# Two transformer blocks in one launch: gate and up of the first block's feed-forward with the tokens stationary

## What is computed

```
def rms_norm(x, g):
    y = xf * lax.rsqrt(jnp.mean(xf * xf, axis=-1, keepdims=True) + NORM_EPS)
    return (y * g)

def swiglu_ffn(h, w_in, w_out):
    gate, up = jnp.split(h @ w_in, 2, axis=-1)
    return (jax.nn.silu(gate) * up) @ w_out

for l in range(DEPTH):                                   # DEPTH = 2
    x = x + 0.5 * swiglu_ffn(rms_norm(x, ffn1_norm_g[l]), ffn1_w_in[l], ffn1_w_out[l])
    ...                                                  # mixing, cross-attention
    x = x + 0.5 * swiglu_ffn(rms_norm(x, ffn2_norm_g[l]), ffn2_w_in[l], ffn2_w_out[l])
```

## Time and profile before

| | us |
|---|---|
| median of 3 runs | 2745.47 |
| profiled execution, its own time | 2742.86 |
| span of its trace | 2740.9 |
| PE busy | 2630.0 |
| DVE busy | 1700.7 |
| ACT busy | 1028.4 |
| four feed-forwards: down(0) of each ended at | 52.0, 635.7, 841.8, 1427.8 |

### The profile page before, as it was taken

How to read it: one execution, slowest core, us unless ns; L and a number is a source line. 1 busy time by engine, 2 the same in 40 slices (tenths; PEclk the granted TensorE clock), 3 DMA queues, 4 the chain that set the end, 5 groups by cost and what they waited for, 6 DMA issues and landing times. The chain is left out here.

```text
span 2740.9 us, 44687 instructions
## 1 busy us (share of the span) xinstructions
PE 2630.0 (96%) x18787; PEld 2324.0 (85%) x18787; DVE 1700.7 (62%) x2283; ACT 1028.4 (38%) x1275; POOL 99.2 (4%) x179
## 2 busy tenths in 40 slices
PE   8999989999989999989999999999999999989999
PEld 7999888989989999779899954355799899737999
DVE  6887655768768877656678822553455455354555
ACT  4335302444343354204443321643333333264333
POOL 2110000001101100000001000000000000000000
PEclk9999989999999999989999999889999999999999
DMA  8775201647766764004557752100355555210452
GB/s 277 261 260 185 93 1 47 200 140 244 261 216 223 264 224 154 16 1 138 171 174 258 260 193 77 46 1 31 127 183 183 199 184 185 78 62 31 140 183 93
DMA packets 279510, 415.63 MB, mean 152 GB/s; under 512 B 10105, under 2 KB 235721, under 8 KB 277698
## 3 DMA queue, kind: packets, MB, share of 16 engines
q1 hardware_dynamic: 260332, 348.16, 38.5%
q0 software_dynamic: 18128, 64.20, 6.8%
q10 hardware_dynamic: 902, 1.15, 0.1%
HBM read 399.82 MB, written 13.65 MB: 151 GB/s over the span
## 5 line engine op out<-in xcount | busy, mean ns | idle before, releaser
L614 PE MATMUL ps<-h_high,w_high 128*128 128x256 f32 x1984 | 567.9, 286 | 17.5 <-DVE w_low L1407 10.5
L616 PE MATMUL ps<-h_high,w_low 128*128 128x256 f32 x2016 | 572.3, 284 | 0.0
L614 PEld LDWEIGHTS ps<-h_high,w_high 128*128 128x128 f32 x1984 | 382.8, 193 | 20.3 <-DVE w_low L1407 11.4
L616 PEld LDWEIGHTS ps<-h_high,w_low 128*128 128x128 f32 x2016 | 389.0, 193 | 0.0
L1407 DVE TENSOR_TENSOR w_low<-ring,w_high 128x2048 fp32r<-128x2048 f32 x132 | 302.3, 2290 | 138.5 <-ACT w_high L1150 138.2
L615 PE MATMUL ps<-h_low,w_high 128*128 128x256 f32 x1312 | 373.4, 285 | 0.0
L2797 DVE TENSOR_TENSOR w_low<-ring,w_high 128x2048 fp32r<-128x2048 f32 x96 | 220.0, 2292 | 240.6 <-ACT w_high L2581 240.4
L1150 ACT ACTIVATE w_high<-ring 128x2048 fp32r<-128x2048 f32 x132 | 252.3, 1915 | 266.7 <-DMA ring<-in_ffn_w_in 147.9
L2581 ACT ACTIVATE w_high<-ring 128x2048 fp32r<-128x2048 f32 x96 | 183.8, 1916 | 331.2 <-PE ps L2260 304.1
L615 PEld LDWEIGHTS ps<-h_low,w_high 128*128 128x128 f32 x1312 | 254.0, 194 | 0.0
L1428 DVE SCALAR_TENSOR_TENSOR mod_acc<-wmod,cond,mod_acc 128x512 f32<-128x512 f32 x336 | 230.8, 748 | 0.0
(11 more groups left out here) (426 smaller groups left out, 5395.0 us busy)
## 6 DMA issues: line engine op xcount, KB each, us to landing
ring<-in_w_mlp SPq DMA_DIRECT2D x96, 1024.0 KB, 5.5
ring<-in_ffn_w_in SPq DMA_DIRECT2D x88, 1024.0 KB, 8.8
wmod<-in_w_mod POOLq DMA_DIRECT2D x96, 512.0 KB, 6.3
ring<-in_ffn_w_out SPq DMA_DIRECT2D x44, 1024.0 KB, 5.1
ring<-in_w_mix_in SPq DMA_DIRECT2D x26, 1024.0 KB, 5.5
ring<-in_xattn_w_kv SPq DMA_DIRECT2D x16, 1024.0 KB, 5.3
mod_scratch<-mod_acc POOLq DMA_DIRECT2D x24, 512.0 KB, 5.5
ring<-mod_scratch SPq DMA_DIRECT2D x12, 1024.0 KB, 6.8
```

The costliest lines, as they stand in the source:

```text
L614: mm(dst, w_hi, x_hi, start=start, stop=False, **more)
L616: return mm(dst, w_lo, x_hi, start=False, stop=stop, **more)
```

## The change

Gate and up are made the other way round. The tokens are stationary (`g_high`, `g_low`, 128 tokens at a time) and the weights move, gate and up side by side, 512 wide. The result has tokens on the partitions, so silu, 1/rms (now a column, `root_col`, one number per partition) and the product with up are done there in two halves of 128 tokens; then PE turns the product back with four transposes (`turn`), ACT makes its high part out of PSUM (`cast`) and DVE its low part (`act_lower`). All 11 steps use x times gain; the normed h of the feed-forward and its splitting fall away, the sums of squares come out as columns. High parts have five buffers: a pair for each half b of gate and up, which must lie so that one access pattern spans both, and one for down (`DOWN_HIGH`, in the place of `h_high`). `sync_program` is not touched.

```diff
+GATE_UP_HIGHS, DOWN_HIGH = ((0, 1), (6, 2)), 7
...
+            def half_products(b, t, k, last=False):
+                out = ps[4 + 2 * b + t].rearrange("p (r n) -> p r n", r=2)
+                toks, cols, s = slice(t * P, (t + 1) * P), slice(k * BLK, (k + 1) * BLK), tiles.slot(0, b)
+                hi, lo = gate_up_high[b][:, :, cols], w_low[:, s:s + 2, cols]
+                mm(out, g_high[:, k, toks], hi, start=(k == 0), stop=False)
+                mm(out, g_high[:, k, toks], lo, start=False, stop=False)
...
+            def turn(i, b):
+                pe.wait_ge(*tiles.act(i, 2))
+                for t in range(2):
+                    for m in range(2):
...
+                        last = nc.tensor.transpose(ps[4 + 2 * b][:, m * T + t * P:m * T + (t + 1) * P],
+                                                   act_tok[:, at:at + P], ident)
...
+            with pe.Fori(1, FFN_STEPS // 2 - 1) as j:
+                gate_up(1, j * 6 + 2)
+                down(j * 2, 0, j * 6 + 4)
+                turn(j * 2 + 1, 1)
+                gate_up(0, j * 6 + 5)
+                down(j * 2 + 1, 1, j * 6 + 7)
+                turn(j * 2 + 2, 0)
...
+                silu(j * 2, 0, j)
+                w_high_part(tiles, 2, 0, j, DOWN_HIGH, (2, 1, j - 1))
+                cast(j * 2, 0)
+                gate_up(0, j + 1, (1, 0, j))
...
+            silu(2 * j + 2, 0, j + 1)
+            w_high_part(tiles, 2, 0, j + 1, DOWN_HIGH, (2, 1, j))
+            cast(2 * j + 2, 0)
...
+            def rest(i, b, down_at, chunk, gate_up_at):
+                k = 4 * b
+                modulate(l, f, chunk, range(k, k + 1))
+                w_low_of(2, b, down_at, DOWN_HIGH)
+                act_lower(i, b)
+                modulate(l, f, chunk, range(k + 1, k + 2))
+                if gate_up_at is not None:
+                    w_low_of(0, b, gate_up_at, GATE_UP_HIGHS[b][0])
+                modulate(l, f, chunk, range(k + 2, k + 3))
+                if gate_up_at is not None:
+                    w_low_of(1, b, gate_up_at + 1, GATE_UP_HIGHS[b][1])
+                modulate(l, f, chunk, range(k + 3, k + 4))
```

More of the change, by code:

```diff
@@ L619, in ffn, with parts @@
             tiles = FfnTiles(l, f)
-            def parts(r, b, t, buffer):
+            def parts(b, t):
                 pe.wait_ge(*tiles.split(t, w_low_ready))
[L624 to L638, removed]
-                    last.then_inc(w_used[tiles.slot(r, 0)].sem, 1)
+                return [ap.rearrange("p (k n) -> p k n", k=2)
+                        for ap in (w_high[DOWN_HIGH], w_low[:, tiles.slot(2, b), :])]
@@ new lines, in half_products @@
+            def half_products(b, t, k, last=False):
[4 more added lines that the diff above has]
+                mm(out, g_high[:, k, toks], lo, start=False, stop=False)
+                if not last:
+                    return mm(out, g_low[:, k, toks], hi, start=False, stop=(k == KD - 1))
+                for r in range(2):
+                    mm(out[:, r, :], g_low[:, k, toks], hi[:, r, :], start=False, stop=(r == 1)
+                       ).then_inc(w_used[tiles.slot(r, b)].sem, 1)
@@ L675, in down, with tiles_half, gate_up @@
-            def down(i, b, t, buffer):
-                hi, lo = parts(2, b, t, buffer)
+                    for t in range(2):
+                        for k in (2 * p, 2 * p + 1):
+                            last = half_products(0, t, k, t == 1 and k == KD - 1)
+                        if t == 0 and p == KD // 2 - 1:
+                            last.then_inc(*tiles_half())
+            def tiles_half():
+                return half_done.sem, 1
+            def gate_up(b, t, between=None):
+                pe.wait_ge(*tiles.split(t + 1, w_low_ready))
+                for half in range(2):
+                    for k in range(KD):
+                        last = half_products(b, half, k, half == 1 and k == KD - 1)
+                    if half == 0:
+                        last.then_inc(*tiles_half())
+                        if between:
+                            between()
@@ new lines, in turn, with down @@
+            def turn(i, b):
+                pe.wait_ge(*tiles.act(i, 2))
+                for t in range(2):
+                    for m in range(2):
+                        at = b * 512 + t * BLK + m * P
+                        last = nc.tensor.transpose(ps[4 + 2 * b][:, m * T + t * P:m * T + (t + 1) * P],
+                                                   act_tok[:, at:at + P], ident)
+                last.then_inc(act_turned.sem, 1)
+            def down(i, b, t, between=None):
+                hi, lo = parts(b, t)
@@ L1183, in ffn, with silu, gate_up @@
-            silu(FFN_STEPS - 1, 0, FFN_STEPS // 2, True)
-            w_high_of(2, 0, FFN_STEPS // 2, 2, (0, 0, FFN_STEPS // 2))
+            def silu(i, b, use):
+                for t in range(2):
+                    act.wait_ge(*(tiles.used(1, b, use) if t else tiles.step(i, half_done)))
+                    at = t * BLK
+                    go(prob[:, b, at:at + BLK], ps[4 + 2 * b + t][:, 0:BLK], SILU, scale=root_col[:, t:t + 1]
+                       ).then_inc(silu_done.sem, 1)
+            def gate_up(b, use, before=None):
+                for r in range(2):
+                    w_high_part(tiles, r, b, use, GATE_UP_HIGHS[b][r], before)
```

295 lines of the change are left out of this document (135 added, 160 removed).

## The result

The changed kernel takes **2842.77 us** (median of four, 2829.82 to 2850.81) against 2745.44 for the kernel before: ratio 1.0349, 95% interval [1.0308, 1.0390], 97 us slower. The forecast of 2808 had the side and the place right; its range ended at 2836, so the time lies outside it.

What follows compares the result with a forecast made beforehand. PE alone was taken to set the 17.28 us step, waiting on a load chain after the change. Steps with clock +54, ends +17 and heads -8 gave +63 us: 2806 profiled, 2808 as median, range 2765 to 2836.

Steps and rivals of the forecast that it cites:

- the 512-wide matmul: PE's gate and up: 0.2144 us each, 10.29 against 11.52 a step; with transposes a step of 16.49, gaining 0.79.
- the landing of up: SP's load of up arrives 13.2 us after a down's end instead of 12.46, delayed by POOL's pieces.
- the clock: PE at 1.2 GHz behind long waits in the steps: 1.5 us for each of four, +6 us a feed-forward.
- DVE's wait for `mod_free`: DVE's k = 0 modulation waits 5.4 us for POOL's store; taken as harmless since DVE has room.
- E10: End of a feed-forward's tenth down, put at 163.0 us after the first down's end, without the clock; before, 155.5.
- the stated recurrence: Each down ends 16.49 us after the later of the last down's end and the one before plus 20.0; +7.5 a feed-forward.
- I take half a piece more: POOL's 512 KB pieces ahead of gate and up take 1.4 us each; half a piece added makes the landing 13.2.
- Ends and heads: Around the feed-forwards: ends +17 us, including 5.0 us waits before the last down; heads -8 us.
- The dearer matmul with more of POOL's traffic in front: Rival in the steps: 512-wide matmuls at 0.2267 us and a 21 us load chain, 2836 us; 8 in 100 including matmul price alone.
- its lesser form: Rival in gate and up: only the 512-wide matmuls dearer, at 0.2267 us, 2820 us; within the same 8 in 100.
- PE still sets the step: Rival in the steps: up lands early enough that PE does not wait, 2726 us; 5 in 100.
- The overlap at 0.12: Rival in gate and up: 512-wide matmuls start 0.12 us apart, gate_up 5.8 us, total 2714; 1 in 100.

Runs made afterwards that it cites:

- experiment 5: Changed kernel with POOL's modulation-weight loads, from the third on, moving 16 columns a row instead of 512: 2807.23 us, ratio 1.0259.
- Experiment 4: Changed kernel with DVE's k = 0 modulation put behind down's and the activation's low parts in every second step: 2833.42 us, ratio 1.0318.
- experiment 8: Kernel before with SP's earlier gate and up loads: 2744.41 us; changed kernel with these, last down's buffer, product first and k = 0 later: 2742.08 us.
- Experiment 6: Changed kernel with twelve extra 256-wide matmuls ahead of the wait before each turn, except first and last step: 2833.48 us, ratio 1.0345.
- SP's order: Changed kernel with SP issuing gate and up of step i+1 ahead of down i: 2749.56 us, ratio 1.0046.
- the three other edits: Onto the changed kernel with SP's earlier loads: last down's high part in buffer 2, product before up's low part, k = 0 modulation later; 2742.08 us.
- experiment 1: Changed kernel with SP issuing gate and up of step i+1 ahead of down i, nothing else moved: 2749.56 us, ratio 1.0046.
- experiment 7: Changed kernel with SP's earlier loads, plus: operand from one stretch, 2751.81 us; each 512-wide matmul as two of 256, 2762.59; one transpose for four, 2739.71.
- e_sp_one_turn: Changed kernel with SP's earlier gate and up loads and one transpose a step instead of four: 2739.71 us, ratio 1.0014.
- e_before_sp: Kernel before, with SP issuing gate and up of the next step ahead of down: 2744.41 us, ratio 0.9997.
- e_sp_last: Changed kernel with SP's earlier gate and up loads and the last down's high part made earlier in buffer 2: 2738.03 us, ratio 0.9995.
- e_sp_contiguous: Changed kernel with SP's earlier loads and the 512 moving columns read from one stretch instead of two: 2751.81 us, ratio 1.0040.
- e_all: Changed kernel with SP's earlier loads, last down's buffer, product ahead of up's low part and k = 0 modulation later: 2742.08 us, ratio 1.0005.
- e_k0_later: Changed kernel with DVE's k = 0 modulation behind down's and the activation's low parts in every second step: 2833.42 us, ratio 1.0318.
- e_last_down: Changed kernel with the last down's high part put in buffer 2 and both its parts made earlier: 2833.08 us, ratio 1.0326.

## Why the prediction was wrong

Three terms of the steps were too small (the 512-wide matmul, the landing of up, the clock), and a fourth, DVE's wait for `mod_free`, was put at nothing. Per feed-forward E1 to E10 was put at 13.5 us more than before and took 25.2 (100.7 / 4): 16.4 of idle PE, and 8.8 more of busy PE, of which 7 are the clock. That is 47 us more than forecast over the four: 16 by the width, some 20 by waits (the landing and `mod_free`), 4 by the clock, and the rest in ends of matmuls and steps of 17.32.

**The width (16 of the 47 us).** "I take 0.2144, since in the f32 rows the excess is gone", with 0.2267 as the upper end. It is 0.231, outside both. The f32 rows were the nearest in width and the wrong ones in kind: beside their 0.2144 a pass fp32r has 17 ns more. The step's own gain of 0.79 is nil. In the stated recurrence, 17.29 in place of 16.49 makes E10 167.0 instead of 163.0 (five of the nine steps carry it on the path, in the others it only shortens the wait): 4.0 a feed-forward. The waits are then 11 a feed-forward; the profile has 16.4. The upper bound had taken the excess per matmul as fixed; nothing in the trace said that it was. The Trainium skill ("TensorE: Matmul & The Clock Gate", Back-to-back issue gap) gives about 216 ns isolated and 131 sustained for 512 columns. This stream, at 231, agrees with neither.

**The landing (some 10).** Up at E + 13.2 was E + 14.0 on average: 0.8 in each of four stalled pairs would be 13, and the waits leave 10 for it beside `mod_free`. "I take half a piece more" should have been a whole one, by experiment 5 (11.2 without POOL's pieces, so by estimate 12.6 with one and 14.0 with two). The pair shown has C = 20.95 where 20.0 was given. The bounds were misread as well, without harm to the sum: "no up landed before E + 11.5" goes by ACT, but in three of the loops' steps ACT starts at E + 11.45 released by PE and not by the load (698.95 for the E of 687.50), and the load itself was there at E + 10.9; the latest of that trace came at E + 16.2.

**`mod_free` (some 10, and the clock behind it).** "DVE has that room" failed. The wait was mostly 6.7 to 8.4 us for 5.4, and with it DVE's chain of the following step came late: in the prediction these steps hardly wait, in the profile eight of them wait 10.7 us in all. Experiment 4 took 10 us of PE's waits away by moving it. Once the loads are early, the room is there again (experiment 8 shows nothing left to gain).

**The clock (4).** 6 a feed-forward for 7: three to five waits of 2.5 us and up, 13 of the 15 followed by a stretch at 1.2 GHz, some of 6.8 us. Experiment 6 took the clock's drops out of the steps and gained 6.6 us in the first feed-forward, net of what it cost. So this term was nearly right.

**Ends and heads: +9 predicted, +3 in the profile.** The wait of 5.0 before the last down is there four times at 5.07 to 5.08. The first head was taken as +2 and is +3.75 (E1 at 55.79 for 52.04), because the paired operand makes the very first gate_up wait for up's low part too, a wait of 8.0 us that ends at 25.53; I had looked at gate_up(1) alone. From E10 to the next E1 the changes are +4.6, -0.5 and +2.2, predicted +1.3, -2.0 and +1.3. Behind the fourth the profile has -7.3 for +6.5, but the profile of before holds a clock stretch there worth 20 us that the profile after lacks (last section): without it this end would be +13 and the ends and heads above the forecast. The two profiles do not settle this term.

**The rivals.** The dearer matmul with more of POOL's traffic in front, at 2836, is the one that came (8 in 100 with its lesser form); its price was 0.2267 and it left out DVE's wait for `mod_free`. I gave it the range's end instead of room beyond it. "PE still sets the step" (2726) is what SP's order makes of the kernel, but at 2749.6, since the gain of 0.79 that it counted on does not exist. The overlap at 0.12 and the operand not read as one did not occur. The side, the place (transposes waiting for the product, released by DVE, with SP's queue at the root) and the last down's 5 us were as predicted.

## What to carry to other kernels

Price a wider matmul by rows of its own data type, and if there is none, let the range reach up to two narrow ones (0.24 here, and the truth was 0.231). Where a change hands PE a consumer that used to be late (here the transposes of the product), look at which loads stand ahead of it in the producer's queue and at whether the load's own wait is the one that it needs: moving two DMA issues past one wait was worth 83 to 93 us, and the three other edits on top of it together 7 to 11. A wait of another engine that costs nothing while its loads are early (7.4 us in experiment 1) can cost once they are late. Here the clock added 28 us to PE's 65 us of waits.

## What the runs showed of the hardware

- fp32r matmuls stand 0.12 us apart at 256 columns and 0.231 at 512, with the moving operand in one stretch or in two; plain f32 matmuls of 512 columns have a weight load every 0.4288 us, 0.2144 a pass if, as the prediction takes it, a load serves two. Why fp32r has 17 ns more is open: one stretch or two is excluded (experiment 7), nothing else was tried, the number of matmuls per weight load neither.
- A transpose of f32 128x128 adds 0.107 us to a step (`e_sp_one_turn`, 0.32 for three), beside the 0.11 of the earlier trace rows.
- The spread between executions of one kernel goes with the clock. Of 25 executions of the kernel before on one chip six took 2730 to 2733 us at a mean granted clock of 0.976 to 0.978, and nineteen 2742 to 2752 at 0.970 to 0.974. One place where profiles differ is the second half's attention: four profiles (the kernel before, `e_before_sp`, `e_sp_last`, `e_sp_contiguous`) show PE at 1.2 GHz for 41 us on end there, three (`e_all`, `e_k0_later`, `e_last_down`) for 24 to 31, and the other seven for 3.4; the changed kernel's has a granted clock of 0.96 over the 44 us that answer to it. What sets it off was not tried. Windows of before:

```profile
1700.00:1768.00 68.00, 62.49 (x152) 22.88 (x150) 32.95 (x65) 39.62 (x69) 0.00 (x0) 0.95 0.16 53
1768.00:1809.00 41.00, 41.00 (x121) 23.53 (x120) 16.73 (x65) 13.32 (x48) 0.00 (x0) 0.50 0.04 16
```

  Half of 41 us is 20: more than many an edit here, so profiles of two kernels should be compared stage by stage.
